# Output projection, norm, first queries and experts in one block, and the experts of two token tiles interleaved head by head

## The reference, cut to what matters

```
merged = (gates[:, :, 0] * (o_a @ wb[:DN_WIDTH])
          + gates[:, :, 1] * (o_b @ wb[DN_WIDTH:DN_WIDTH + SWA_OUT])
          + gates[:, :, 2] * (o_c @ wb[DN_WIDTH + SWA_OUT:]))
x = x + merged @ w_out[l]
x = x + _peer(_rmsnorm(x, norm_ffn[l]), peer_query[l], peer_subkeys[l], peer_up[l], peer_down[l])
...
q = (xt @ w_query).reshape(n, PEER_HEADS, 2, PEER_DKEY // 2)          # in _peer: 8 heads, two halves each
s = jnp.einsum('nhpd,pkd->nhpk', q, subkeys)                          # 128 keys for each half
s1, i1 = lax.top_k(s[:, :, 0], PEER_TOPK)                             # top 16 of each half
s2, i2 = lax.top_k(s[:, :, 1], PEER_TOPK)
cand = s1[..., :, None] + s2[..., None, :]                            # 256 sums, top 16 of them
expert = i1[ic // 16] * PEER_KEYS + i2[ic % 16];  gate = softmax(best)
act = gelu(einsum('nd,nhkd->nhk', xk, w_up[expert])) * gate           # each token: 8 x 16 = 128 experts of 16384
down = einsum('nhk,nhkd->nd', act, w_down[expert])
```

## Time and profile before

| | |
|---|---|
| median of 3 runs | 5640.61 us (5632.93 to 5645.94) |
| the profiled execution's own time | 5640.35 us |
| its span | 5638.3 us |
| mean granted clock of PE | 0.954 |
| busy: PE, DVE, ACT, POOL | 85%, 53%, 22%, 27% |
| moved by DMA | 1432.13 MB, mean 254 GB/s |

### The profile page before, as it was taken

One profiled execution on the slowest core, in us unless ns is written; L12 is line 12 of the kernel. 1 busy time (PEld: TensorE's weight loads), 2 busy tenths in 40 slices (PEclk: granted clock), 3 DMA queues, 4 the chain that ended last, 5 costly groups with the idle time before them and its releaser, 6 DMA issues. The chain is left out here.

```text
span 5638.3 us, 50965 instructions
## 1 busy us (share of the span) xinstructions
PE 4807.7 (85%) x17538; PEld 2850.4 (51%) x17538; DVE 2983.9 (53%) x7244; ACT 1250.1 (22%) x3129; POOL 1542.7 (27%) x1422
## 2 busy tenths in 40 slices
PE   7889999999987777777788899999899877777776
PEld 5775777756543223322267757777565322333221
DVE  4522212215679999655455222132156799996554
ACT  2211220103223333211122112211122233332111
POOL 0311100002444444443304111000034444444332
PEclk9989998999999999999999899999999999999999
DMA  2212241317999999999812222423189999999997
GB/s 98 75 55 76 65 143 63 126 31 279 388 404 421 421 421 415 414 421 421 349 65 76 66 68 67 142 76 122 31 324 387 405 421 421 421 418 419 421 419 305
DMA packets 338619, 1432.13 MB, mean 254 GB/s; under 512 B 27388, under 2 KB 156278, under 8 KB 190442
## 3 DMA queue, kind: packets, MB, share of 16 engines
q0 software_dynamic: 177376, 1268.07, 55.3%
q1 hardware_dynamic: 155054, 157.63, 8.8%
q10 hardware_dynamic: 5932, 3.19, 0.2%
HBM read 1400.16 MB, written 49.44 MB: 257 GB/s over the span
## 5 line engine op out<-in xcount | busy, mean ns | idle before, releaser
L2307 PE MATMUL ps<-early,diag 128*128 128x512 f32 (+1 forms) x3328 | 1572.9, 619 | 377.7 <-ACT diag L2238 377.4
L2158 POOL DMA_INDIRECT early<-in_peer,ids x832 | 909.0, 1093 | 1769.7 <-PE ps L2307 1166.9
L2307 PEld LDWEIGHTS ps<-early,diag 128*128 128x128 f32 (+1 forms) x3328 | 609.3, 190 | 1297.4 <-issue 665.0
L2182 DVE SCALAR_TENSOR_TENSOR early<-early,rows 128x1024 f32<-128x1024 f32 x832 | 1004.4, 1223 | 375.0 <-DMA early<-in_peer,ids 374.3
L2307 PE MATMUL ps<-late,diag 128*128 128x512 f32 (+1 forms) x1280 | 614.8, 626 | 187.2 <-ACT diag L2238 187.1
L2238 ACT ACTIVATE diag<-consts_sb,weight 128x128 f32<-128x128 f32 (+1 forms) x1152 | 392.6, 388 | 650.1 <-DVE weight L2192 639.7
L2307 PEld LDWEIGHTS ps<-late,diag 128*128 128x128 f32 (+1 forms) x1280 | 230.2, 189 | 569.8 <-ACT diag L2238 313.1
L2158 POOL DMA_INDIRECT late<-in_peer,ids x320 | 349.1, 1091 | 464.3 <-PE ps L2307 435.5
L2182 DVE SCALAR_TENSOR_TENSOR late<-late,rows 128x1024 f32<-128x1024 f32 x320 | 386.8, 1224 | 159.0 <-DMA late<-in_peer,ids 158.6
L1186 PE MATMUL ps<-hT,gate_ring 128*128 128x288 f32 x1536 | 416.4, 427 | 0.0
L2230 ACT ACTIVATE gel<-dot 128x2 f32<-128x2 f32 x576 | 117.4, 204 | 1254.6 <-DVE early L2182 853.7
(11 more groups left out here) (350 smaller groups left out, 5660.0 us busy)
## 6 DMA issues: line engine op xcount, KB each, us to landing
gate_ring<-in_w_in POOLq DMA_DIRECT2D x48, 512.0 KB, 4.7
ring<-in_w_in SPq DMA_DIRECT2D x12, 1536.0 KB, 7.1
slot<-in_w_branch SPq DMA_DIRECT2D x16, 1152.0 KB, 6.1
ring<-in_w_in SPq DMA_DIRECT2D x8, 2048.0 KB, 9.2
late<-in_peer_query SPq DMA_DIRECT2D x32, 512.0 KB, 7.4
gate_rows<-gate_out POOLq DMA_DIRECT2D x48, 288.0 KB, 2.4
slot<-gate_rows SPq DMA_DIRECT2D x16, 864.0 KB, 8.0
early<-in_peer,ids POOLq DMA_INDIRECT x832, 21.1
```

Of the source, the lines that this page charges most:

```text
L2158: pool.indirect_dma_start(place(q), None, table_rows, bass.IndirectOffsetOnAxis(ap=ids[:, n, c:c + 1], axis=0)).then_inc(s.pair[PLACE[q]], 16)
L2182: nc.vector.scalar_tensor_tensor(out=up, in0=up, scalar=1.0, in1=rows[:, n, :], op0=ALU.mult, op1=ALU.mult, accum_out=dot[:, i % 2, k:k + ...
L2307: ins = nc.tensor.matmul(g.ps[0:r, 2 * (n % 2) + m, :], diag[:, q % DIAGS, 0:r], place(q)[:, D + m * 512:D + (m + 1) * 512], start=False, ...
```

## The change

The three blocks become one. A class `Output` holds what merge_stage did, and the norm goes under the projection tile by tile. Tiles are taken in the order 4, 0, 1, 2, 3; when a tile's two halves are added to `x`, ACT squares it, DVE and ACT make its root, DVE scales it, and PE transposes it behind the products of the next tile. The transposed halves are copied by ACT and DVE, one each. The loads of the keys and of the query weights go out as soon as the branch products are done.

Query 0 is now half 0 of unit 0 and query 1 half 0 of unit 1. They need tiles 0 to 2 only. Behind them `first_scores` makes the scores of tile 0 alone for units 0 and 1, and after those tile 3 is transposed.

The experts of tiles 0 and 1 take turns head by head: 16 gathers of tile 0, 16 of tile 1, next head. The queries of a head are spread over two such steps, before every other group, and routing parts go behind groups 0 to 3 of each step in both tiles. The 8 places last to gather 199 and not 103.

```
+    ORDER = (4, 0, 1, 2, 3)
...
+        for v, n in enumerate(self.ORDER):
+            if v >= 2:
+                pe.wait_ge(s.x_added, 2 * (v - 1))
...
+            if n == 3:
+                keys()
+            if v:
+                self.turn(pe, self.ORDER[v - 1])
...
+            act.wait_ge(s.x_added, 2 * v + 2)
+            if v:
+                act.wait_ge(s.squared, v)
+            nc.scalar.activation(self.junk[0:r], g.x[0:r, n, :], ACT.Square, accum_out=self.ss[0:r, n:n + 1]).then_inc(s.squared, 1)
+            if n == 3:
+                keys()
+            if v:
+                self.turned(act, nc.scalar.copy, self.ORDER[v - 1], 0)
...
+            nc.vector.scalar_tensor_tensor(out=self.rows[0:r, n, :], in0=g.x[0:r, n, :], scalar=root, in1=self.gam[0:r, :],
+                                           op0=ALU.mult, op1=ALU.mult).then_inc(s.normed, 1)
+        self.turned(dve, nc.vector.tensor_copy, self.ORDER[-1], 1)
...
+TOGETHER = 2
+HEADS = [(n, h) for h in range(PH) for n in range(TOGETHER)] + [(n, h) for n in range(TOGETHER, TILES) for h in range(PH)]
...
-EXTENDED = 13 * EARLY
+EXTENDED = 25 * EARLY
...
-        if todo and (i >= groups[0] or i % STEP < 4):
+        if todo and (i > TILE_END[TOGETHER - 1] or i % STEP < 4):
             slots[i] = todo.pop(0)
...
+    for step in range(PH - 2):
+        i, u = step * TOGETHER * STEP, 2 * (step + 2)
+        for a in range(4):
+            asking[i + 2 * a] = ("query", 2 * u + a)
+        asking[i + 9], asking[i + 11] = ("scores", u), ("scores", u + 1)
+    halves = [(0, 0), (1, 0), (0, 1), (1, 1)] + [(u, a) for u in range(2, NQ) for a in range(2)]
...
+            out.scalar(act, keys)
+            query(0)
+            query(1)
+            first_scores(0)
+            first_scores(1)
+            out.turned(act, nc.scalar.copy, 3, 0)
...
+            out.tensor(pe, keys)
+            pe.wait_ge(s.hT_a, out.place(2) + 1)
+            pe.wait_ge(s.hT_b, out.place(2) + 1)
+            query(0)
+            pe.wait_ge(s.act_c, 1)
+            query(1)
+            pe.wait_ge(s.x_added, out.added(3))
+            first_scores(0)
+            first_scores(1)
+            out.turn(pe, 3)
+            pe.wait_ge(s.hT_a, TILES)
+            pe.wait_ge(s.hT_b, TILES)
+            query(2)
+            query(3)
+            scores(0)
+            scores(1)
```

More of the change, by code:

```diff
@@ L1916, in loaded @@
         eng.wait_ge(self.g.s.merge_in[j % MERGE_RING], 32 * (self.l * uses + j // MERGE_RING + 1))
[L1919 to L1956, removed]
-                    for k in range(KT):
-                        last = nc.tensor.matmul(g.ps[:, 4 + u % 4, :], merged[:, k, cols(n)], w_out[:, k, i * 512:(i + 1) * 512],
-                                                start=k == 0, stop=k == KT - 1)
-                    last.then_inc(s.pe_b, 1)
-                pe.wait_ge(s.dve_c, 5)
@@ L2108, with score_expert_stage @@
 TURN = [PLACE[:q].count(PLACE[q]) for q in range(PAIRS)]
-def score_expert_stage(nc, g, t, l, rows, sc, sc0, ids, gates, router, late, w_q, sb):
+def score_expert_stage(nc, g, t, l, rows, sc, sc0, ids, gates, router, late, w_q, out, sb):
     s = g.s
     table_rows = t["peer"].rearrange("l e d -> (l e) d")
-    groups = [COUNT[n] // GROUP for n in range(TILES)]
     landed = lambda q: 16 * (l * USES[PLACE[q]] + TURN[q] + 1)
@@ L2163, in _ @@
             link = Link(dve, s.link_dve)
+            out.vector(dve, link)
             opened = []
@@ L2239, in _ @@
                                          scale=weight[:, i % 2, k:k + 1]).then_inc(s.diagonal, 1)
[L2240 to L2245 removed]
+                if i in asking:
+                    kind, u = asking[i]
+                    if kind == "query":
+                        query(u)
+                    else:
                         scores(u)
[L2247 to L2250 removed]
+                for done in range(TILES - 1):
+                    if i == TILE_END[done] + 4:
+                        copy_x(done)
             copy_x(TILES - 1)
@@ L2273, in scores, with keys @@
                 last.then_inc(s.pe_b, 1)
-            pe.wait_ge(s.loaded, 16)
-            for i in range(2):
-                last = nc.tensor.transpose(g.ps[:, 7, i * P:(i + 1) * P], late.keys[:, i, :], ident(g))
-            last.then_inc(s.pe_c, 1)
-            pe.wait_ge(s.act_c, 1)
-            for u in range(4):
+            def keys():
+                pe.wait_ge(s.loaded, 16)
+                pe.wait_ge(s.x_added, out.added(2))
+                for i in range(2):
+                    last = nc.tensor.transpose(g.ps[:, 5, i * P:(i + 1) * P], late.keys[:, i, :], ident(g))
+                last.then_inc(s.pe_c, 1)
```

326 lines of the change are left out of this document (205 added, 121 removed).

## The result

| | before | after |
|---|---|---|
| median of 4 runs | 5637.72 us | 5572.39 us |
| lowest to highest | 5632.93 to 5645.94 | 5567.46 to 5578.33 |
| the profiled execution's own time | 5640.35 | 5569.33 |
| its span | 5638.3 | 5567.5 |
| mean granted clock of PE | 0.954 | 0.954 |

The ratio is 0.9885, with a 95% interval of 0.9869 to 0.99. The changed kernel is 1.15% faster. The forecast was 5578, inside a range of 5555 to 5622.

The account below looks back on a forecast made before the run. PE was taken to bound tile 0 and DMA the experts behind it. Per layer 25.1 + 20.3 - 8 - 6 = 31.4 us, 62.8 in all, gave 5578 us, 8-in-10 range 5555 to 5622.

Parts of the forecast that it names:

- What bounds the kernel: Expert part: PE bounds tile 0 (gathers at 387 GB/s), DMA at 421 behind it; 20.3 us lost a layer.
- Projection and norm, to the first gather: From the projection's first product (T): query 0 at T+70.7, first gather at T+92, 25 us earlier.
- To the first freed place: Start of expert loop: loop at T+112.4, ninth gather 28.3 us behind the first, about 8 us lost.
- Rounds of 32 gathers: Gathers up to 199: DMA becomes the bound (82.2 us against PE's 73.5); shortage of 8 places costs 6 us a layer.
- my worst group: Expert group with routing part and PE behind from queries: 15.3 us needed against 14.2 available, about 1 us short.
- The sum: Whole layer: 25.1 + 20.3 - 8 - 6 = 31.4 us gained, 62.8 in all.
- The clock: PE in rounds: 73.5 us kept; at the 0.91 clock's price 81.3, still under DMA's 82.2.
- Eight places as the bound: Rival, gathers 24 to 199: 8 places limit the rate; 5666 at 378 GB/s (0.08), about 5641 at 387 (0.06).
- Only the head start kept: Rival, rounds: PE's clock falls, most of 20.3 stays lost, only the loop's 14.5 us a layer gained; 5612, chance 0.15.
- The loop doesn't suffer: Rival, start and rounds: their losses of 8 and 6 us are nearly nothing, gain 45 a layer; 5550, chance 0.06.
- The head start does not come: Rival, new block: a wait on DVE or ACT holds the routing; each under 3 us, inside the range, no own chance.

Follow-up runs that it names:

- e2: The kernel before with only the interleaving of tiles 0 and 1 head by head, 8 places to gather 199: 5611.3 us, ratio 0.996 to the kernel before.
- e1: The changed kernel with the one block but tile 0 alone again, 8 places to gather 103: 5602.19 us, ratio 0.9944 to the kernel before.
- e6: The changed kernel with each round's queries moved off the groups with routing parts, scores later too: 5588.66 us, ratio 0.9914 to the kernel before.
- e4: The changed kernel with queries and scores of units 2 and 3 moved into the expert loop's groups 0 to 7, later rounds eight groups later: 5564.3 us, 0.9878.

## Why the prediction was right

**What bounds the kernel: right.** PE in tile 0, DMA behind it. e2 gave PE slack, with the same 8 places held for longer, and the 387 became 408; e1 moved the first gather 26.7 us and PE let 17.4 and 15.9 of them through.

**Projection and norm, to the first gather: right.** T+92 was forecast and T+90.5 measured. Query 0 starts at T+69.5 (70.7 forecast), DVE begins the routing at T+80.0 behind its copy of tile 3's half (81.5), and the routing takes 10.2 us (10.2). The first two queries took 8.0 us, the sum's 7.9. Most of the 1.2 us at query 0 are the transposes between the projection's products: 0.64, 0.88 and 0.88 us from start to start for tiles 4, 0 and 1, where the sum had 1.3 each. The waits on `x_added` cost nothing, as said: between the projection's first product and 1260 PE has no idle time.

**To the first freed place: right.** The loop starts at T+110.6 (112.4), the ninth gather is 27.95 us behind the first (28.3). The start's loss was put at 8 us. From the windows: 38.6 us at 338 are 13.0 MB or 31.0 us at 421, so 7.6 lost less 3.2 for the landing, 4.4; 1.7 more up to 1340 (379) and 1.1 up to 1360 (398): 7.2.

**Rounds of 32 gathers: the mechanism right, the size too small.** 6 us were forecast. 17.4 - 7.2 = 10.2 were lost. (e2, with the start of before, lost 12.3 in the same way, for which 8 to 12 were expected.) I had counted every routing part as a quarter of 10.2, 2.6 us. In the trace of the changed kernel the parts are unequal. DVE in the fourth part of a routing, from its first instruction to its last and the group's weight behind it; then PE (start, us):

```profile
1572.50 0.17 DVE L2126 TENSOR_SCALAR two<-pos 128x16 uint32<-128x16 uint32 x1
...
1575.80 0.23 DVE L2137 TENSOR_SCALAR ids<-num,before 128x16 uint32<-128x16 f32 x1
1575.94 0.15 DVE L2279 TENSOR_TENSOR weight<-gel,gates 128x2 f32<-128x2 f32 x1
```

```profile
1571.02 3.60 PE L2427 MATMUL ps<-early,diag 128*128 128x512 f32 x8
1576.58 5.40 PE L2427 MATMUL ps<-early,diag 128*128 128x512 f32 x8 [1.97 <-ACT diag L2341]
1581.81 4.04 PE L2363 MATMUL ps<-late 128*128 128x288 f32 x16
1585.69 7.03 PE L2427 MATMUL ps<-early,diag 128*128 128x512 f32 x16
```

The fourth part takes 3.5 us (1572.50 to 1576.0). PE idles 1.97 us for the diagonal behind it, then takes 5.40 for a group of 3.70, and a query of 3.88 follows. So places come 4.7 and 4.9 us after POOL wants them, and the next 20 us move 361 GB/s. That is 0.9 us more for the part and 1.7 for the group than my worst group had. It is read from the trace at this place; that it makes up the 4 us in all was argued, not tried.

**The sum.** 26.7 + 20.3 - 7.2 - 10.2 = 29.6 a layer, from windows; 31.8 and 30.6 were measured at the end, 31.4 forecast. So that the total fits to within 1 us a layer is in part luck: the rounds cost 4.2 more than forecast, the first gather and the start gave 2.4 more. The rest comes out when gathers are counted and not bytes. The stretch holds 96 gathers more than before and takes 523.8 - 288.7 = 235.1 us more, 4.0 less than the 239.1 that they take at 421; behind it are 96 fewer, and that part, 1209.8 us before and 969.6 now, is 240.2 shorter, 1.1 more than 239.1. 26.7 + 4.0 + 1.1 = 31.8. In layer 2 it is 26.3 + 4.7 - 0.4 = 30.6. So five sixths of the gain are the earlier first gather; the interleaving gives 4 to 5 us a layer of its own (20.3 - 8 - 6 = 6.3 forecast) and lets the earlier start through.

**The clock.** I kept PE's price at full clock against the price of the rows at 0.91. The stretch reads 0.98, nearer to mine. It is not free of work at half clock: the window of 10 us around the one above reads 0.83, the mean of stretches at 2.4 and at 1.2 GHz. The rule that I had weighed against the change (the Trainium skill, page "TensorE: Matmul & The Clock Gate", section "HAM oscillation — how this bites in real kernels") is seen in kind in e6, where PE had bursts between waits (0.92 in 1439 to 1460), and is a small part of the time here: the stretch reads 0.98.

**The rivals.** Eight places as the bound: refuted by e2 and by the 410 GB/s. But the margin was thinner than a chance of 0.14 for both of its cases suggests: break-even was 388, seven places give 395 and six give 369, at which the kernel is slower than before. Only the head start kept: refuted as to its time, since it counted the 14.5 us of PE's loop and 26.7 came through. Its premise came nearer than that: of the 20.3 us lost in 104 gathers, 17.4 are still lost, though in 200. The loop doesn't suffer: refuted by the ninth gather, 27.95 behind. e4 took that hole away, and little came of it (5564 and 5570), so 5550 wasn't reached by that order either. The head start does not come: refuted.

## What to carry to other kernels

When gathers pace a stage but an engine behind them has no gap, ask which of the two an earlier start feeds: with PE the bound only its own loop's start counted (some 16.6 of 26.7 us), and with DMA the bound the first gather did, less what DMA lost behind it (20 us). Don't trust a plan that shows free groups on one engine: moving the queries off the routing, to groups that looked free, cost 8 to 11 us a layer (e6). And a hole removed at the start is not won at the end: e4 took away the 7 us that DMA lost there and ended 2.4 us a layer earlier in the traces, which the times can't tell from nothing.
